# Five residual sums moved from VectorE to accumulating transfers, and one pair's forms moved into a block step

## What is computed

```python
merged = sigmoid(gate_a_m) * (o_a @ w_up_a[l]) + sigmoid(gate_b_m) * (o_b @ w_up_b[l])
x = x + merged @ w_out[l]
h2 = rms_norm(x, g_mlp[l])
x = x + jnp.square(jax.nn.relu(h2 @ w_ff1[l])) @ w_ff2[l]
```

## Time and profile before

| | |
|---|---|
| median of 3 runs | 742.1 us (741.59 to 742.56) |
| profiled execution: time | 741.73 us |
| profiled execution: span | 740.0 us |
| granted TensorE clock, mean | 1.000 |
| TensorE, matmul busy | 731.7 us (99%) |
| TensorE, weight load busy | 651.4 us (88%) |
| VectorE busy | 585.3 us (79%) |
| ScalarE busy | 437.7 us (59%) |
| GpSimd busy | 177.1 us (24%) |
| moved by DMA | 71.00 MB, mean 96 GB/s |

### The profile page before, as it was taken

One profiled execution on the slowest core, in us unless ns is written; L12 is line 12 of the kernel. 1 busy time (PEld: TensorE's weight loads), 2 busy tenths in 40 slices (PEclk: granted clock), 3 DMA queues, 4 the chain that ended last, 5 costly groups with the idle time before them and its releaser, 6 DMA issues.

```text
span 740.0 us, 12690 instructions
## 1 busy us (share of the span) xinstructions
PE 731.7 (99%) x4686; PEld 651.4 (88%) x4686; DVE 585.3 (79%) x1079; ACT 437.7 (59%) x803; POOL 177.1 (24%) x192
## 2 busy tenths in 40 slices
PE   9999999999999999999999999999999999999998
PEld 9998977877997778777888899999999888799997
DVE  5478889769986877666767988988887788897987
ACT  7768377756767897555356555566556544533341
POOL 3110336523555545300012422222220000000000
PEclk9999999999999999999999999999999999999999
DMA  9621221111111111102533333333332332323332
GB/s 336 252 81 50 76 87 58 57 29 58 53 54 47 49 58 58 57 31 85 199 115 96 105 114 105 96 97 104 114 115 86 100 100 86 108 92 114 115 123 77
DMA packets 22861, 71.00 MB, mean 96 GB/s; under 512 B 2448, under 2 KB 5648, under 8 KB 22544
## 3 DMA queue, kind: packets, MB, share of 16 engines
q1 hardware_dynamic: 22800, 70.19, 30.5%
HBM read 68.08 MB, written 2.10 MB: 95 GB/s over the span
## 4 chain that ended last, share of the span: by engine, by line
PE 83%; DVE 8%; ACT 5%; issue 2%; DMA 1%; POOL 0%; DVEq 0%; SPq 0%; POOLq 0%
PE psum L2143 23%; PE psum L2145 22%; PE psum L2144 22%; PE psum L2151 5%; PE psum L2340 4%; PE psum L2317 2%; PE psum L2318 2%; DVE w_lo L1481 1%; DMA x2T<-in_xT 1%; ACT w_hi L1056 1%; DVE prob L1695 1%; ACT h L1056 1%; ACT q_st L1056 1%; DVE x2T L1848 1%; PE psum L2158 1%
## 5 line engine op out<-in xcount | busy, mean ns | idle before, releaser
L1056 ACT ACTIVATE w_hi<-stage 128x512 fp32r<-128x512 f32 (+4 forms) x149 | 114.7, 777 | 30.6 <-PE psum L2145 26.8
L2143 PE MATMUL psum<-hT_hi,w_hi 128*128 128x256 f32 (+1 forms) x324 | 113.5, 350 | 0.8 <-DVE q_st L1637 0.6
L2144 PE MATMUL psum<-hT_lo,w_hi 128*128 128x256 f32 (+1 forms) x324 | 107.3, 331 | 0.0
L2145 PE MATMUL psum<-hT_hi,w_lo 128*128 128x512 f32 (+1 forms) x264 | 90.6, 343 | 0.0
L1481 DVE TENSOR_TENSOR w_lo<-stage,w_hi 128x1024 fp32r<-128x1024 f32 (+4 forms) x58 | 56.8, 985 | 41.3 <-ACT w_hi L1056 37.1
L1056 ACT ACTIVATE w_hi<-s_sum 128x1024 fp32r<-128x1024 f32 x46 | 48.7, 1060 | 54.3 <-PE psum L2145 52.0
L2144 PE MATMUL psum<-a_lo,w_hi 128*128 128x512 f32 (+1 forms) x224 | 77.0, 344 | 0.0
L1243 ACT ACTIVATE prob<-prob,neg_max 128x128 f32<-128x128 f32 (+3 forms) x96 | 53.8, 560 | 35.4 <-DVE neg_max L1695 34.7
L1020 POOL TENSOR_TENSOR w_lo<-stage,w_hi 128x512 fp32r<-128x512 f32 x46 | 59.6, 1300 | 36.2 <-ACT w_hi L1056 36.0
L2143 PE MATMUL psum<-t_hi,w_hi 128*128 128x256 f32 x240 | 67.9, 283 | 0.0
L2144 PE MATMUL psum<-t_lo,w_hi 128*128 128x256 f32 x240 | 67.9, 283 | 0.0
(11 more groups left out here) (316 smaller groups left out, 2042.4 us busy)
## 6 DMA issues: line engine op xcount, KB each, us to landing
stage<-in_panels SPq DMA_DIRECT2D x104, 512.0 KB, 3.6
xT_in<-in_xT SPq DMA_DIRECT2D x8, 260.0 KB, 5.1
x_in<-in_x SPq DMA_DIRECT2D x4, 512.0 KB, 7.3
phi<-in_phi SPq DMA_DIRECT2D x2, 1024.0 KB, 6.8
x2T<-in_xT SPq DMA_DIRECT2D x1, 2048.0 KB, 9.0
stage<-in_panels SPq DMA_DIRECT2D x8, 212.0 KB, 5.1
stage<-in_panels SPq DMA_DIRECT2D x4, 408.0 KB, 3.1
stage<-in_panels SPq DMA_DIRECT2D x4, 384.0 KB, 5.0
```

Of the source, the lines that this page charges most:

```text
L1056: return nc.scalar.activation(dst, src, ACT.Copy, scale=scale)
L2143: mm(dst, a_h, b_h, start=start, stop=False)
L2144: mm(dst, a_h, b_l, start=False, stop=False)
L2145: return mm(dst, a_l, b_h, start=False, stop=stop)
```

## The change

The five VectorE adds become five transfers issued from GpSimd that add their source to their destination (`accum_op`), from `y_plain` into `x2T`, each with a semaphore of its own; they are issued after GpSimd's last other work, first the three for output half 0 (`i` = 4, 6, 7), then the two for half 1. `add_first` waits for the three or for the two. The forms of pair 14 move from panel 12 to panel 13, and those of pair 15 from panel 14 into block step 0: ScalarE's `round_forms(15)` stands there between `round_first` and `round_s12` of the next step, VectorE's `scale_pair` and `sum_forms` between `low_first` and `low_s`, and `low_forms` behind `low_last` of step 1. Two form buffers move to other addresses, and the buffer for transfers' descriptors grows from 1024 to 8192 bytes.

```diff
-FORMS_PLAIN = {3: 8, 5: 9, 6: 10, 8: 11, 9: 12, 11: 13, 12: 14, 14: 15}
-Y_ADDED_AT = {1: [0], 2: [2, 3], 5: [4], 6: [6]}
+FORMS_PLAIN = {3: 8, 5: 9, 6: 10, 8: 11, 9: 12, 11: 13, 13: 14}
+FORMS_STEP = {0: 15}
...
-        t_form_at = [35 * K, 46 * K] + [Z + k * K for k in (75, 86, 129)] + [54 * K] + [Z + k * K for k in (3, 137)]
+        t_form_at = [35 * K, 46 * K] + [Z + k * K for k in (75, 86, -12)] + [54 * K, Z + 3 * K, Z - 8 * K]
         form_sum_at = [at + 4 * K for at in t_form_at[:-1]] + [Z + 12 * K]
+        form_sum_at[4] = Z + 129 * K
...
-        y_added = sem("y_added")
+        y_added = {i: sem(f"y_added{i}") for i in (0, 2, 4, 6, 7)}
...
+            def add_y(i):
+
+                b, n = Y_ORDER[i], 2 if i < 6 else 1
+                wait_drained(pool, ("y", Y_ORDER[i + n - 1]))
+                src = y_plain[:, i:i + n, :] if i < 7 else y_plain_end[:, None, :]
+                nc.gpsimd.dma_start(x2T[:, b:b + n, :], src, accum_op=ALU.add).then_inc(y_added[i], 16)
+
+            for i in (4, 6, 7, 0, 2):
+                add_y(i)
...
                 if n + 1 < NSTEPS:
                     round_first(n + 1)
+                if m in FORMS_STEP:
+                    round_forms(FORMS_STEP[m])
                 if n + 1 < NSTEPS:
                     round_s12(n + 1)
                     round_s34(n + 1)
...
-                ve.wait_ge(y_added, 5 if half else 3)
+                for i in (0, 2) if half else (4, 6, 7):
+                    ve.wait_ge(y_added[i], 16)
...
                 low_last(n)
+                if m - 1 in FORMS_STEP:
+                    low_forms(FORMS_STEP[m - 1])
...
                 if n + 1 < NSTEPS:
                     low_first(n + 1)
+                if m in FORMS_STEP:
+                    i = FORMS_STEP[m]
+                    scale_pair(i)
+                    sum_forms(i)
...
-                for b in Y_ADDED_AT.get(m, []):
-                    add_y(b)
...
-    nc = bacc.Bacc("TRN2", target_bir_lowering=False, num_devices=1, dynamic_dma_scratch_size=1024)
+    nc = bacc.Bacc("TRN2", target_bir_lowering=False, num_devices=1, dynamic_dma_scratch_size=8192)
```

More of the change, by code:

```diff
@@ L467, in hybrid_layer @@
         rstd_bc = place_small("rstd_bc", [P, S])
+        late_small = small
         q_scale = place_small("q_scale", [P, H])
@@ L592, in hybrid_layer @@
         b_at = [32 * K, 43 * K] + [Z + k * K for k in (72, 83, 126, 120, 0, 123)]
-        t_form_at = [35 * K, 46 * K] + [Z + k * K for k in (75, 86, 129)] + [54 * K] + [Z + k * K for k in (3, 137)]
+        t_form_at = [35 * K, 46 * K] + [Z + k * K for k in (75, 86, -12)] + [54 * K, Z + 3 * K, Z - 8 * K]
         form_sum_at = [at + 4 * K for at in t_form_at[:-1]] + [Z + 12 * K]
+        form_sum_at[4] = Z + 129 * K
+        assert Z - 12 * K >= late_small
         form_b = [place(f"form_b{i}", [P, 3, half_s], at, F32R) for i, at in enumerate(b_at)]
@@ L601, in hybrid_layer @@
         y_plain_end = place("y_plain_end", [P, S], Z + 94 * K)
-        assert base + Z + 141 * K <= nc.sbuf_usable_end
+        assert base + Z + 133 * K <= nc.sbuf_usable_end
         bank_full = [sem(f"bank_full{b}") for b in range(8)]
@@ L2010, in scale_y @@
                 drained(tt_op(y_scaled(i), ps, rstd_bc[:, :], ALU.mult), ("y", b))
[L2012 to L2020, removed]
             def two(ps):
```

## The result

The changed kernel took 743.2 us (median of 10 runs, 742.79 to 744.1) against 741.69 for the kernel before, measured beside it: ratio 1.0021, 95% interval 1.0011 to 1.003. The forecast was 743.5 us. The profiled execution spans 741.2 us, 1.2 more than the one of before, and took 742.95 us.

What follows compares the result with a forecast made beforehand. TensorE alone was taken to pace the stage, at 10.08 us a step; -0.54 + 1.61 + 0.40 = +1.47 us, taken as 1.4, on the 742.1 us median gave 743.5 us, forecast 742.8 to 744.7, whole range 741.6 to 746.0.

Steps and rivals of the forecast that it cites:

- The sum, +1.47, taken as 1.4: Whole kernel: -0.54 in the plain stage, +1.61 in step 1 and +0.40 at step 2's start.
- Plain stage, -0.54: FF2's plain stage, panel 12: TensorE's wait for a_lo goes once pair 14's forms move to panel 13; 0.54 us won.
- First gap, 1.53 with 0.08 for the restart: Before product 2 of step 1: TensorE waits for s_lo, late through pair 15's forms; 1.53 us, with the restart 1.61.
- Second gap, 0.32: Start of step 2: TensorE waits for w_lo, late behind pair 15's low_forms on VectorE; 0.32 us, 0.40 with its restart.
- The five adds, 0: Steps 1, 2, 5 and 6: taking 5.0 us of adds off VectorE wins 0, as no step shows a TensorE stall.
- The transfers, 0: Block steps: the five accumulating transfers, 2.1 MB beside the panel loads, were taken to add no time.
- panel loads of over 5 us: Sign of a wrong forecast: panel loads slower than 5 us, where 3.6 us was usual.
- a load at half rate: Panel load beside the transfers takes 7.2 us; step 2's second panel, issued 665.4, lands at 672.6, just in time.
- Rival (b): Steps 0 to 3: transfers hold up panel loads, 1.4 us a step, 744.9 to 746.3 us; chance 0.22 with GpSimd slowing VectorE.
- GpSimd's issues beside VectorE, 0: Block steps: at worst each of five issues slows one VectorE instruction by 0.94 us, 4.7 us in all; taken as 0.
- The wait in add_first, 0: VectorE at about 690 and 730 us: transfers are in by 678 and 699, so it waits 0.
- bounds of 3.6 and 41 us: Transfer times: 3.6 us like a 512 KB panel load, or 41 us for all 2.1 MB at 51 GB/s.

Runs made afterwards that it cites:

- paced transfers: Transfers issued one at a time, at product 4 of steps 0, 1, 2, 4, 5: changed kernel 743.21 us; with the forms as before the change 741.75 us.
- transfers alone: Changed kernel with the forms of pairs 14 and 15 back in panels 12 and 14, five transfers kept: 746.15 us, ratio 1.0053 to the kernel before.
- forms one step later: Changed kernel with transfers issued one at a time and pair 15's forms in block step 1, not 0: 743.05 us, ratio 1.0014 to the kernel before.
- roundings first: Changed kernel with ScalarE's part of pair 15's forms behind the two roundings of the sums in step 0: 745.22 us, ratio 1.0044 to the kernel before.
- panel 15: Changed kernel with pair 15's forms wholly in the plain stage's panel 15, ahead of the block steps: 745.71 us, ratio 1.0052 to the kernel before.

## Why the prediction was right, and where it was lucky

- **The sum, +1.47, taken as 1.4.** Measured +1.5. That the time is 0.3 us under the forecast is the kernel before, 741.69 us beside the changed one, where the forecast stood on 742.1.
- **Plain stage, -0.54.** Measured -0.61. The stall went for the reason given, split_act(12) ends at 630.58 (630.8 was said).
- **First gap, 1.53 with 0.08 for the restart.** Measured 1.53 and 0.11. Every link of the chain came 0.2 to 0.35 us before the time said, as this execution's plain stage began 0.26 earlier: scale_pair 663.06 for 663.27, form_t 665.96 for 666.17, round_s12 666.92 for 667.13, low_s 667.99 for 668.23, product 2 at 669.27 for 669.61. Taking ScalarE's part out of the way removed it; moving it a step later moved it.
- **Second gap, 0.32.** Measured 0.35, and 0.30 with paced transfers, whose load is in time, so by the cause that was given.
- **The five adds, 0.** Shown with the paced transfers: 0.9997 of before with them off VectorE.
- **The transfers, 0.** This is the term that came out right only because another loss covered it, and so by luck. The prediction named panel loads of over 5 us as a sign of being wrong, and that sign came: 5.9 us in the median. It priced a load at half rate at 7.2 us and had the one of step 2 land "just in time"; it took 7.8 us and was in time by 0.1. That was the forms' delay: in the kernels without it the same transfers cost 3.2 to 4.2 us, with the clock's part. Rival (b) got 0.22 as something that would come on top of the forecast; it should have been told as a loss that the forecast's own stall hides. It gave step 3 as the first to pay; in those kernels it was step 2, whose load took 7.8 to 9.0 us.
- **GpSimd's issues beside VectorE, 0.** The bound of 0.94 us for each VectorE instruction beside an issue was not needed: the sums between 659 and 662 us took 0.68 to 0.69 us, beside issues that went on to 662. The Trainium skill's page SBUF — State Buffer ("Who interferes with whom") says that a VectorE instruction with two SBUF inputs contends with GpSimd's reads and not with its writes. The trace doesn't show what an issue reads or writes in SBUF; it agrees in so far as five issues left these sums as they were.
- **The wait in add_first, 0.** VectorE's sum after the transfers waits for ScalarE there, not for a transfer. The five transfers took 5.9 to 12.5 us each, and the last had landed by about 673, inside the bounds of 3.6 and 41 us for all.

## What to carry to other kernels

When an engine's share of a job is inserted into a queue written by hand, look at what it waits for from the other engine, and at what stands behind it in its own queue: here three instructions of ScalarE waited for VectorE's newest work, and two roundings that had all they needed stood behind them. Price transfers that are "off the path" by what they do to the loads already in flight, and ask that question again with each other stall of the forecast taken away, since one loss can hide a larger one. The work that the change moved fits into VectorE's 5.5 us idle before the first block step: with it there, and the adds where they were, the kernel took 740.97 us, the lowest of all, though its interval ends at 1.0, so only its missing gaps are certain.

## What the runs showed of the hardware

- These accumulating transfers are dearer in engine time than the loads: in the changed kernel's stretch from 655 to 680 us 2.10 MB of them took 46.7% of the 16 engines and 2.62 MB of loads 30.5%, 1.9 times as much for each byte; one at a time, in the paced kernel with the transfers alone, 0.79 MB took 17.3% and 2.65 MB of loads 34.2%, 1.7 times. They also go from SBUF to SBUF and are issued by GpSimd; which of the three makes them dearer wasn't tried. One at a time, 512 KB land in 4.9 us, 256 KB in 3.2; with five issued within 6 us they take 9.5 and 6.6 in the median, and a load beside them up to 9.0 instead of 3.6. The Trainium skill's page DMA: Bandwidth & Descriptors ("Issuing engines are not separate DMA queues") says that all queues run on the same 16 engines and interleave; these runs agree.
- TensorE's clock turned a late load into a dearer one. In the traces, after gaps of 1.53 us (changed kernel) and 1.46 us (forms one step later) the granted clock stayed at 1.00 (2.4 GHz); after 1.94 us (roundings first) it fell to 0.50 (1.2 GHz) some 0.94 us behind the restart, and after 2.90 us (panel 15) and 3.13 us (transfers alone) it stood at 0.50 from the restart; each time for 3.2 to 3.4 us, an estimated 1.4 us lost by the starts of 0.21 us in place of 0.12. These are single executions. Two of the five of the transfers alone had a mean clock of 0.999 and 1.000, from which one such stretch would take 0.002 (3.2 us at half the clock, of 745), so they paid little of this or nothing; that the length of the gap alone decides isn't shown.
